# A two-layer encoder on one core: turns of the FFN's closing norm regrouped, first attention weights split early, last head's halves summed in PSUM

## The reference, cut to what matters

```python
for i in range(DEPTH):                       # DEPTH = 2
    mix = diff_attention(...) if i % 2 == 0 else neighborhood_attention(...)
    x = layer_norm(alpha * x + mix, ln_g[i, 0], ln_b[i, 0])
    ff = conv_ffn(x, ...)
    x = layer_norm(alpha * x + ff, ln_g[i, 1], ln_b[i, 1])
# neighbourhood attention, 16 heads of 64:
qkv = x @ w_qkv + b_qkv
s = q_row . k_sel + bias ; p = softmax(s) ; o = p @ v_sel ; out = o @ w_o + b_o
```

## Time and profile before

| | us |
|---|---|
| median of 3 runs | 2770.74 (2770.68 to 2773.01) |
| the profiled execution's own time | 2769.38 |
| its span in the profile | 2767.6 |
| TensorE (PE) busy | 2648.8, 96% |
| VectorE (DVE) busy | 1912.8, 69% |
| GpSimd (POOL) busy | 1685.6, 61% |
| ScalarE (ACT) busy | 1195.8, 43% |
| mean granted clock of TensorE | 0.985 of full |

### The profile page before, as it was taken

How to read it: one execution, slowest core, us unless ns; L and a number is a source line. 1 busy time by engine, 2 the same in 40 slices (tenths; PEclk the granted TensorE clock), 3 DMA queues, 4 the chain that set the end, 5 groups by cost and what they waited for, 6 DMA issues and landing times. The chain is left out here.

```text
span 2767.6 us, 35849 instructions
## 1 busy us (share of the span) xinstructions
PE 2648.8 (96%) x13043; PEld 2213.4 (80%) x13043; DVE 1912.8 (69%) x2487; ACT 1195.8 (43%) x1789; POOL 1685.6 (61%) x1188
## 2 busy tenths in 40 slices
PE   8999999989899999999989999998889999999998
PEld 7888888877778888888868888887767888888887
DVE  3767666674687666777774777777477777666768
ACT  3554544462253333333444555555425333333333
POOL 3444444364586677777835666655467776677775
PEclk9999999999999999999999999998899999999999
DMA  3000110235111221211231212111401211221212
GB/s 124 29 29 23 30 30 21 64 94 175 33 39 46 61 61 46 61 46 46 76 102 43 54 45 53 45 47 52 171 12 55 61 46 46 61 61 46 60 47 92
DMA packets 213004, 161.73 MB, mean 58 GB/s; under 512 B 36139, under 2 KB 194939, under 8 KB 212859
## 3 DMA queue, kind: packets, MB, share of 16 engines
q1 hardware_dynamic: 212715, 159.29, 19.4%
q10 hardware_dynamic: 144, 0.52, 0.1%
HBM read 136.19 MB, written 23.59 MB: 58 GB/s over the span
## 5 line engine op out<-in xcount | busy, mean ns | idle before, releaser
L1494 POOL TENSOR_TENSOR ff_Rlf<-raw_weights 128x512 f32<-128x512 f32 x210 | 329.8, 1583 | 54.3 <-PE ff_ph L1591 33.0
L1501 POOL TENSOR_TENSOR ff_Rl<-ff_Rlf,ff_Rh 128x512 fp32r<-128x512 f32 x210 | 311.5, 1500 | 24.8 <-ACT ff_Rh L1757 24.8
L1501 POOL TENSOR_TENSOR ff_Rl<-raw_weights,ff_Rh 128x512 fp32r<-128x512 f32 x84 | 156.8, 1877 | 253.0 <-ACT ff_Rh L1757 253.0
L1757 ACT ACTIVATE ff_Rh<-ff_Rlf 128x512 fp32r<-128x512 f32 x210 | 130.4, 630 | 365.4 <-POOL ff_Rlf L1494 365.1
L1591 PE MATMUL ff_ph<-XTh,ff_Rh 128*128 128x512 f32 x672 | 262.4, 391 | 7.8 <-POOL ff_Rl L1501 7.5
L1591 PE MATMUL ff_ph<-XTh,ff_Rl 128*128 128x512 f32 x672 | 261.6, 389 | 0.0
L1591 PE MATMUL ff_ph<-XTl,ff_Rh 128*128 128x512 f32 x672 | 261.5, 389 | 0.0
L1638 PE MATMUL ff_po<-ff_WDh,WH 128*128 128x512 f32 x624 | 244.6, 392 | 0.0
L1638 PE MATMUL ff_po<-ff_WDh,WL 128*128 128x512 f32 x624 | 243.0, 389 | 0.0
L1638 PE MATMUL ff_po<-ff_WDl,WH 128*128 128x512 f32 x624 | 242.9, 389 | 0.0
L1859 DVE TENSOR_TENSOR X<-ff_po,X 128x512 f32<-128x512 f32 x288 | 191.4, 684 | 66.0 <-PE ff_po L1638 66.0
(11 more groups left out here) (358 smaller groups left out, 7457.3 us busy)
## 6 DMA issues: line engine op xcount, KB each, us to landing
raw_weights<-in_ffn_w_in SPq DMA_DIRECT2D x168, 256.0 KB, 3.3
ff_WDlf<-in_ffn_w_out SPq DMA_DIRECT2D x40, 512.0 KB, 4.1
raw_weights<-in_attn_w_qkv SPq DMA_DIRECT2D x24, 512.0 KB, 3.8
raw_weights<-in_na_w_qkv SPq DMA_DIRECT2D x24, 512.0 KB, 4.2
rpb_rows<-da_rows SPq DMA_DIRECT2D x2, 3840.0 KB, 26.5
na_B<-rpb_rows SPq DMA_DIRECT2D x32, 224.0 KB, 4.4
wo_oraw<-heads_t SPq DMA_DIRECT2D x10, 512.0 KB, 4.8
da_E<-in_x SPq DMA_DIRECT2D x8, 512.0 KB, 6.1
```

Source lines behind the costliest of these rows:

```text
L1494: nc.gpsimd.tensor_tensor(out=Rf[:, i % SLOTS], in0=quad(*a), in1=quad(*b), op=op).then_inc(quad_sum, 1)
L1501: nc.gpsimd.tensor_tensor(out=Rl[:, i % SLOTS], in0=src, in1=Rh[:, i % SLOTS].bitcast(F32), op=ALU.subtract).then_inc(quad_low, 1)
L1757: nc.scalar.activation(Rh[:, i % SLOTS], src, ACT.Copy).then_inc(quad_high, 1)
```

## The change

Three edits. (1) In the first FFN, TensorE turns tiles 0 and 1 together behind r = 11 instead of tile 0 behind r = 9 and tile 1 behind r = 11, and ScalarE and VectorE take both there. Tile 6 is closed by `scale` on ScalarE and `shift` on GpSimd and no longer by `finish`; `finish` of tile 7 goes between the low parts of tiles 4 and 5. Ahead of `shift(3)` GpSimd no longer waits for the gain of tile 5. (2) The first two weight tiles of neighbourhood attention are split during the end of FFN 0 into places of X whose tiles are stored and turned (X tiles 0, 1, 2): ScalarE rounds both, GpSimd makes the first low part. The next stage reads its weights at this address (`first_w`), TensorE's first projection waits for nothing, and the second low part alone is left for VectorE at the stage's start. Every x tile's store has a semaphore of its own. (3) In the last head pair every product with V is made with the map's high and low part as two matmuls of half the columns into the same place, so the two column halves are summed in PSUM; ScalarE copies 64x256 and one VectorE instruction of 64x256 writes `last_head`.

```diff
@@ ffn_stage @@
-        FINISHED = (4, 5, 6, 7)
+        FINISHED = (4, 5, 6, 7) if last_layer else (4, 5, 7)
-        TURNS = {4: [0], 5: [1], 6: [2, 3], 7: [4, 5, 6, 7]}
-        ENDS = {t: [] for t in range(TT)} | ({6: [4, 5], 7: [6, 7]} if last_layer else {5: [4], 6: [5], 7: [6, 7]})
-        LOWS = {4: [0], 5: [1], 6: [2, 3], 7: [4, 5, 6, 7]}
+        TURNS = {4: [], 5: [0, 1], 6: [2, 3], 7: [4, 5, 6, 7]}
+        ENDS = {t: [] for t in range(TT)} | ({6: [4, 5], 7: [6, 7]} if last_layer else {5: [4], 6: [5], 7: []})
+        LOWS = TURNS
-        y_stored = [m.sem(f"y_stored{i}") for i in range(2)]
+        y_stored = [m.sem(f"y_stored{t}") for t in range(TT)]
+        first_high, first_low = m.sem("first_high"), m.sem("first_low")
...
@@ GpSimd @@
             for t in range(TT):
                 if 2 <= t <= 5:
-                    pool.wait_ge(norm.gained, t + 1)
+                    if t < 5:
+                        pool.wait_ge(norm.gained, t + 1)
                     norm.shift(pool, t - 2)
+                if t == 6 and not last_layer:
+                    pool.wait_ge(first_high, 1)
+                    pool.wait_ge(y_stored[1], 16)
+                    pool.wait_ge(norm.turned, 2)
+                    nc.gpsimd.tensor_tensor(out=first_w[:, 0, 1], in0=wraw[:, 0].rearrange("p (k n) -> p k n", k=KT),
+                                            in1=first_w[:, 0, 0].bitcast(F32), op=ALU.subtract).then_inc(first_low, 1)
                 norm.root(pool, t)
+                if t == 6 and not last_layer:
+                    norm.shift(pool, t)
@@ ScalarE @@
                 if t >= 4 and not last_layer:
                     for u in LOWS[t]:
                         norm.high(act, u)
+                if t == 5 and not last_layer:
+                    prefetch.wait(act)
+                    act.wait_ge(y_stored[0], 16)
+                    nc.scalar.activation(first_w[:, 0, 0], wraw[:, 0].rearrange("p (k n) -> p k n", k=KT),
+                                         ACT.Copy).then_inc(first_high, 1)
+                if t == 6 and not last_layer:
+                    act.wait_ge(y_stored[2], 16)
+                    act.wait_ge(norm.turned, 3)
+                    nc.scalar.activation(first_w[:, 1, 0], wraw[:, 1].rearrange("p (k n) -> p k n", k=KT),
+                                         ACT.Copy).then_inc(first_high, 1)
+                    norm.scale(act, t)
@@ VectorE @@
                     for u in LOWS[t]:
+                        if u == 5:
+                            norm.finish(dve, TT - 1)
                         norm.low(dve, u)
@@ neighbourhood_stage @@
-        wh = m.sb("wh", [P, 3, KT, P], F32R)
-        wl = m.sb("wl", [P, 3, KT, P], F32R)
+        m.sb("w_place", [P, 3, 2, KT, P], F32R)
+        wh, wl = first_w[:, :, 0], first_w[:, :, 1]
...
@@ TensorE @@
-                    if h == 0 and j == 0:
-                        pe.wait_ge(w_high, 1)
-                    elif j % 2 == 0:
-                        pe.wait_ge(w_low, 3 * h + j // 2 + 1)
+                    if j % 2 == 0 and (h or j):
+                        pe.wait_ge(w_low, 3 * h + j // 2)
...
+            def weigh_summed(h, s):
+                c, qt = s // QT, s % QT
+                out = pb[(8 * h + s // 2) % 2][:, (s % 2) * P:(s % 2 + 1) * P]
+                p = PT[:, (STEPS * h + s) % 3]
+                v0 = lows[qt] * GW // P
+                whole = range(1, KB) if wraps[qt] else range(KB)
+                for k in whole:
+                    for a in range(2):
+                        last = nc.tensor.matmul(out, V[:, v0 + k, c].rearrange("p a d -> p (a d)"), p[:, k, a],
+                                                start=(k == whole[0] and a == 0),
+                                                stop=(k == KB - 1 and a == 1 and not wraps[qt]))
+                if wraps[qt]:
+                    for r, v in enumerate((V[:, v0, c], Vx[:, qt - WRAP0, c])):
+                        at = slice(r * GW, (r + 1) * GW)
+                        for a in range(2):
+                            last = nc.tensor.matmul(out[:, at], v.rearrange("p a d -> p (a d)"), p[:, 0, a, at], start=False,
+                                                    stop=(r == 1 and a == 1))
+                last.then_inc(pv_done, 1)
...
+                if h + 1 == H:
+                    return weigh_summed(h, s)
@@ ScalarE @@
-            for j in range(3):
-
-                if j == 2:
-                    nc.scalar.preload_act_table(ACT.Exp)
-                    act.wait_ge(w_in[0], 16)
-                nc.scalar.activation(wh[:, j], wraw[:, j % 2], ACT.Copy).then_inc(w_high, 1)
+            nc.scalar.preload_act_table(ACT.Exp)
+            act.wait_ge(w_in[0], 16)
+            nc.scalar.activation(wh[:, 2], wraw[:, 0], ACT.Copy).then_inc(w_high, 1)
...
+                n = 2 * P if h + 1 == H else 4 * P
+                nc.scalar.activation(otmp[:, 0:n], pb[pair % 2][DH:P, 0:n], ACT.Copy).then_inc(o_half, 1)
@@ VectorE @@
+                if h + 1 == H:
+                    at = s % QT // 2 * 2 * P
+                    place = tail[(s // QT) * DH:(s // QT + 1) * DH, at:at + 2 * P]
+                    nc.vector.tensor_tensor(out=place, in0=pb[i % 2][0:DH, 0:2 * P], in1=otmp[:, 0:2 * P],
+                                            op=ALU.add).then_inc(o_out, 1)
+                    return
...
-            for j in range(3):
-                dve.wait_ge(w_high, j + 1)
+            for j in range(1, 3):
+                if j == 2:
+                    dve.wait_ge(w_high, 1)
                 nc.vector.tensor_tensor(out=wl[:, j], in0=wraw[:, j % 2], in1=wh[:, j].bitcast(F32),
                                         op=ALU.subtract).then_inc(w_low, 1)
```

More of the change, by code:

```diff
@@ L927, in __init__ @@
         TT, self.D = X.shape[1:]
+        self.shared = [t for t in range(TT) if t not in finished]
         self.tp = [turned_psum[t % len(turned_psum)] for t in range(TT)]
@@ L953, in wait_y @@
         else:
-            eng.wait_ge(self.shifted, t + 1)
+            eng.wait_ge(self.shifted, self.shared.index(t) + 1)
     def load(self, sp):
@@ L1284, in ffn_stage @@
 def ffn_stage(nc, name, w_in_d, b_in, conv_w, conv_b, w_out, b_out, g, b, x_out, X, XTh, XTl, ident, alpha, last_layer,
-              wraw, WH, WL, WHf, next_tiles):
+              wraw, WH, WL, WHf, next_tiles, first_w):
     D = w_in_d.shape[0]
@@ L1461, in _ @@
                 norm.wait_y(sp, t)
-                sp.dma_start(x_out[t * P:(t + 1) * P, :], X[:, t]).then_inc(y_stored[t % 2], 16)
+                sp.dma_start(x_out[t * P:(t + 1) * P, :], X[:, t]).then_inc(y_stored[t], 16)
             if last_layer:
@@ L1466, in _ @@
                     sp.wait_ge(norm.finished_y, len(FINISHED) + half)
-                    sp.dma_start(x_out[(TT - 1) * P:TT * P, at], X[:, TT - 1, at]).then_inc(y_stored[half], 16)
-                sp.wait_ge(y_stored[0], 16 * (TT // 2 + 1))
-            else:
-                sp.wait_ge(y_stored[0], 16 * (TT // 2))
-            sp.wait_ge(y_stored[1], 16 * (TT // 2))
+                    sp.dma_start(x_out[(TT - 1) * P:TT * P, at], X[:, TT - 1, at]).then_inc(y_stored[TT - 1], 16)
+            for t in range(TT):
+                sp.wait_ge(y_stored[t], 32 if last_layer and t == TT - 1 else 16)
         @block.gpsimd
@@ L2120, in load @@
             def load(h, j):
-                sp.wait_ge(w_low, 3 * h + 1 if j == 2 else 3 * h - j)
+                if h or j < 2:
+                    sp.wait_ge(w_low, 3 * h if j == 2 else 3 * h - j - 1)
                 sp.dma_start(wraw[:, j % 2], column_tile(w_qkv, h * P + j * D)).then_inc(w_in[j % 2], 16)
@@ L2159, in _ @@
                 if h + 2 == H:
-                    sp.wait_ge(w_low, 3 * H)
+                    sp.wait_ge(w_low, 3 * H - 1)
                     prefetch.start(sp)
@@ L2174, in split @@
                 pool.wait_ge(proj_done, 6 * h + 2 * j - 4)
-                pool.wait_ge(w_low, 3 * h + j)
+                pool.wait_ge(w_low, 3 * h + j - 1)
                 nc.gpsimd.tensor_scalar(wh[:, j], wraw[:, j % 2], 1.0, 1.0, ALU.mult, ALU.mult).then_inc(w_high, 1)
-                pool.wait_ge(w_high, 3 * h + j + 1)
+                pool.wait_ge(w_high, 3 * h + j - 1)
                 nc.gpsimd.tensor_tensor(out=wl[:, j], in0=wraw[:, j % 2], in1=wh[:, j].bitcast(F32),
@@ L2248, in _ @@
             split(1, 0)
-            double_k(0, 0, w_low, 4)
+            double_k(0, 0, w_low, 3)
             pad_q(0, 0)
@@ L2292, in project @@
                 for i in range(i0, i0 + n):
-                    k, p = (i % KT, i // KT) if h == 0 and j == 0 else (i // 3, i % 3)
-                    if h == 0 and j == 0 and i == 2 * KT:
-                        pe.wait_ge(w_low, 1)
+                    k, p = i // 3, i % 3
                     w, x = ((wh, XTh), (wh, XTl), (wl, XTh))[p]
@@ L2439, in take_o @@
                     act.wait_ge(o_out, pair)
```

(10 more changed lines are left out.)

9 lines of the change are left out of this document (5 added, 4 removed).

## The result

| | us |
|---|---|
| changed kernel, median of 5 runs | 2784.26 (2765.20 to 2785.82) |
| kernel before, median of the 5 runs beside it | 2770.74 |
| ratio, after to before | 1.0037, 95% interval 1.0024 to 1.0049 |
| profiled execution, own time and span | 2785.82, 2784.0 |

The forecast was 2766.3 with a range of 2761 to 2771; the median lies 18 us above the forecast and 13.3 above the upper end of the range. In both together nine of ten runs lie between 2782.9 and 2786.3, and one at 2765.2. So this kernel has two times, some 19 us apart. The kernel before shows one (2768.6 to 2774.5 in all its undisturbed runs of this study). The rest of this document is about where the two come from. The ratio counts the short run too; the plain quotient of the medians is 2784.26 / 2770.74 = 1.0049.

What follows compares the result with a forecast made beforehand. TensorE, busy 96% of the span, was taken as the bound, so only its idle or low-clock places could give time. 0.3 + 1.1 + 3.0 = 4.4 us off the median 2770.74 gave 2766.3, range 2761.0 to 2771.0.

Steps and rivals of the forecast that it cites:

- part 3: Last head pair: products summed in PSUM shorten VectorE's path while TensorE pays for narrower matmuls; 3.0 us gain taken.
- 0.5 (low clock in both places): Last head pair: lower bound of the gain, 0.5 us, if the clock is low at 1935 to 1938 and at the end.
- +0.5 to +5 us: Last head pair: bounds of the gain, 0.5 with low clock in both places, 5 us at the full clock.
- The 3.0 of the forecast: Last head pair: gain taken between the bounds, 3.0 us, with the clock good in one of the two places.
- The slower rival: Last head pair: summed products meet the low clock most of the time; 7 us slower, 2777.8 us; chance 0.05.
- the clock rival: Neighbourhood stage's start and last head: the full clock holds; 8.2 us gain, 2762.5 us; chance 0.25.
- Part 1: End of the first FFN: regrouped turns and tile 6 shared out end the stage earlier; 0.3 us gain.
- Part 2: Neighbourhood stage's start: weights split early, so TensorE's first projection waits for nothing; 1.1 us gain.
- the zero that I took for the clock there: Neighbourhood stage's first projection: gain from a clock that might not fall, bounds 0 and 1.8 us, taken as 0.
- Step 6: Last head pair: smaller copy and single add shorten the path from copy to next bias by 1.0 us per two steps.
- Eight products: Last head pair: eight matmuls of 128 columns take 0.9 us at the full clock.
- ten at the low clock: Last head pair's wrapped steps: ten matmuls cost 2.2 us at the low clock instead of 1.1.

Runs made afterwards that it cites:

- e2: Kernel before with only the summed products of the last head pair added: eight runs at 2763.39 to 2767.19 us, three at 2783.36 to 2784.97, median 2766.38.
- e14: Changed kernel without the summed products and with the closing norm's turns one tile at a time again: 2768.15 us, ratio 0.9991.
- e1: Changed kernel with the last head pair's summed products undone (256-column products, old copy, two adds): 2771.32 us, ratio 1.0003.
- e6: Changed kernel without the summed products, VectorE making low parts of tiles 0 and 1 before the finish of tile 4: 2767.84 us, ratio 0.9988.
- e12: Changed kernel with the old turns of tiles 0 and 1, summed products kept: five runs at 2762.62 to 2764.09 us, seven at 2778.47 to 2785.82.
- e7: Changed kernel with four unread 512-column matmuls in each of last-head steps 6 to 8, and low parts of tiles 0 and 1 before tile 4's finish: 2768.10 us.
- e4: Changed kernel with four unread 512-column matmuls added in each of steps 6, 7 and 8 of the last head pair: 2765.94 us, ratio 0.9982.
- e15: e12 with four unread 512-column matmuls added in each of the last head's steps 4 to 8: 2765.83 us, ratio 0.9983.
- e13: e2 with four more 512-column matmuls ahead of the neighbourhood stage's second projection: five runs at 2781.69 to 2789.45 us, ratio 1.0052.

## Why the prediction was wrong

**The step that failed** is in part 3, the lower bound of the last head: "0.5 (low clock in both places)". It took the low clock as something that comes at a place, stays for its 3 us and goes, because the profile of before showed it so at 1935 to 1938. The change made this end uncertain. Before, the products had 256 columns; with 128 the clock stayed at 0.50 for some 50 us in the changed kernel's profile. So the term was not +0.5 to +5 us but one of two: 5.2 to 5.4 won when the clock stays up (e2, short group) or 13.7 lost when it falls and stays (the changed kernel). Why it stays down in one execution and not in another is open. The profile of before held a warning that the prediction read only as a price: at the end of the last head the clock was low from about 1956 to 1969, through eight products of 256 columns and waits between them.

```profile
1954.00:1958.00 4.00, 3.26 (x18) 2.93 (x18) 3.21 (x4) 3.59 (x7) 3.04 (x3) 0.70 0.00 0
1958.00:1962.00 4.00, 2.04 (x8) 1.78 (x8) 2.86 (x6) 1.00 (x2) 2.48 (x1) 0.50 0.01 2
```

The 3.0 of the forecast lay between two cases and matched neither.

**The price was there, its chance was not.** The slower rival had the mechanism and the size of a pair right: 8.3 us for two steps at 1.2 GHz, measured 8.15. It let this happen twice and gave it 0.05. In fact, in the changed kernel's profile, it held for all steps from 7 on and the tail, and nine of ten runs were as long. I should have asked of each place with a low clock what brought the clock back there before, and whether the change leaves that in place. My argument against the clock rival, that halved matmuls stream the same columns, spoke about columns alone and was used only against a gain.

**Point by point.**
- Part 1 forecast a stage end 0.3 us earlier; it came 0.24 later. The order of events was right to 0.05 us up to the second turn: no wait ahead of turns 0 and 1, then a wait for VectorE's low part behind a finish held up by a shift (3.33 us). Wrong was what came behind that idle time of nearly 3 us: the clock fell and the transposes cost 1.5 us more. The wait of 0.76 us for ScalarE's high part of tile 4 had no term either. The joint turn and the rest of the first edit were costed as one, and they pull apart: the rest wins 1.7 us of stage end (e14), and the joint turn costs 2.8 us (e1 less e14, each against its own kernel before) and eats it.
- Part 2 forecast 1.1, measured 3.43 - 2.40 = 1.03. The 24 matmuls of that projection took 7.7 us in the profiles of both kernels, as the zero that I took for the clock there says; in e1, e14 and e6 they took 7.5, 7.2 and 7.0.
- Parts 1 and 2 together come to -0.5 us (e1) against a forecast of 1.4. The changed kernel's profile alone would have said 0.8; the fall at the last turn, seen in e1's profile, makes the difference.
- Part 3 at the full clock: forecast bound 5, measured 5.2 to 5.4, of which at least 1.5 is the clock that did not fall and not the shorter path. Step 6 forecast 1.0 sooner, measured 1.06. Eight products forecast 0.9, measured 0.92; ten at the low clock forecast 2.2, measured 2.14 (from 1967.63 to 1969.77).

The Trainium skill (TensorE: Matmul & The Clock Gate, "Back-to-back issue gap") gives about 81 ns for a matmul of 128 columns. The trace shows 0.92 / 8 = 0.115 us at the full clock, so the trace disagrees, and choosing the row of before over the skill was right.

## What to carry to other kernels

Where a stretch of a profile has a low granted clock, look for what raised it again, and ask whether the change keeps it; a price at the low clock counts for as long as the clock stays down in the new kernel, not for as long as the profile of before had it. A change that splits matmuls into narrower ones should be costed at both clock levels over the whole stretch until the next wide matmuls. And where a kernel's runs fall in two groups, count the runs of each: one profile, or one median, shows only one of the two.

## What the runs showed of the hardware

- TensorE busy for all of every window does not by that alone get its full clock. In the changed kernel it was so busy from 1934 to 1978, at 0.50 from about 1935 on; in e12 from 1922 to about 1964. In e12 it then came back among the same narrow products, with no wide matmuls added, so these are not the only way out. What brought it back there stays open, as does why it came back within step 4 in e7 and not in e12.
- Twelve matmuls of 512 columns, whose result nobody reads and which cost 0.23 us each at the full clock, made the changed kernel 18 us shorter (e4). Twenty of them left no long run where seven of twelve had been long (e15 and e12).
- The clock fell behind waits of quite different length: 1.34 us (changed kernel, 1.2 us later), 2.10 us (before, 0.4 us later) and 2.75 us (changed kernel, second turn). It stayed up behind waits of 1.67 us (before, 5 us earlier) and of 1.09 and 0.98 us (e2).
- A kernel that was long in three of eleven runs (e2) was long in five of five with 0.9 us more work over 400 us ahead of the stretch (e13), on another chip.
- An instruction of VectorE with both operands in SBUF, 0.13 us behind one of GpSimd of 2.39 us, took 3.33 us instead of 1.28. The prediction had read this mechanism from the rows of before.
